# Rounding the next stage's first weights inside the stage in front of it, and modulations in six units

## What is computed

```
mod = silu(c) @ w_ada[l] + b_ada[l]                  # 6 x 1024: shift, scale, gate, twice
h   = layernorm(x) * (1 + sc1) + sh1
proj = h @ w_in                                      # attention, GLA, convolution and gate parts
y = (g_att * att(..) @ w_att_o + g_gla * gla(..) @ w_gla_o + g_conv * conv(..) @ w_conv_o) @ w_out
x = layernorm(ALPHA * x + g1 * y)
x = layernorm(ALPHA * x + g2 * ffn(layernorm(x) * (1 + sc2) + sh2))
```

## Time and profile before

| | |
|---|---|
| median of the runs | 2996.16 us |
| the profiled execution, its span | 3002.65, 3000.9 us |
| PE busy | 2813.7 us (94%) |
| DVE, ACT, POOL busy | 1306.7, 1310.4, 1382.3 us |
| granted TensorE clock, mean | 0.976 |
| read from HBM | 355.51 MB |

### The profile page before, as it was taken

How to read it: one execution, slowest core, us unless ns; L and a number is a source line. 1 busy time by engine, 2 the same in 40 slices (tenths; PEclk the granted TensorE clock), 3 DMA queues, 4 the chain that set the end, 5 groups by cost and what they waited for, 6 DMA issues and landing times.

```text
span 3000.9 us, 45357 instructions
## 1 busy us (share of the span) xinstructions
PE 2813.7 (94%) x19004; PEld 2414.5 (80%) x19004; DVE 1306.7 (44%) x2717; ACT 1310.4 (44%) x2204; POOL 1382.3 (46%) x646
## 2 busy tenths in 40 slices
PE   7999998899999999998999999999998899988998
PEld 5778876688876788886878799989986799876898
DVE  3777857532333211104676753332137442174440
ACT  3254433323424422224464346454454465445563
POOL 3432030244431534443531267668762488632786
PEclk9999999999998999999999999999999999998999
DMA  6332022132324343334320245435543255432454
GB/s 237 121 106 81 29 78 82 46 119 92 119 84 157 121 139 128 119 99 166 124 71 22 64 133 156 148 129 182 182 120 120 78 183 175 137 121 84 137 180 123
DMA packets 103555, 359.48 MB, mean 120 GB/s; under 512 B 11127, under 2 KB 17527, under 8 KB 102841
## 3 DMA queue, kind: packets, MB, share of 16 engines
q1 hardware_dynamic: 103352, 356.60, 37.0%
HBM read 355.51 MB, written 1.05 MB: 119 GB/s over the span
## 4 chain that ended last, share of the span: by engine, by line
PE 79%; DVE 9%; ACT 6%; POOL 3%; DMA 1%; issue 1%; SPq 0%; ACTq 0%; DVEq 0%
PE PS L358 79%; POOL RINGL L2516 2%; ACT AR L1161 2%; DVE AR L1795 1%; ACT AR L1690 1%; ACT WH L1141 1%; DVE AR L1799 1%; DMA RING<-w_ada_in 1%; ACT L1161 1%; DVE AR L1956 1%; DVE SM L1795 1%; ACT XT L1161 1%; DVE SM L2029 1%; DVE AR L2400 1%; DVE ARR L1795 1%
## 5 line engine op out<-in xcount | busy, mean ns | idle before, releaser
L2516 POOL TENSOR_TENSOR RINGL<-RING,WH 128x1024 fp32r<-128x1024 f32 (+1 forms) x554 | 1300.7, 2361 | 1507.3 <-ACT WH L1141 1506.6
L358 PE MATMUL PS<-HTR,WH 128*128 128x256 f32 (+2 forms) x2736 | 876.0, 321 | 0.0
L1141 ACT ACTIVATE WH<-RING 128x1024 fp32r<-128x1024 f32 (+1 forms) x554 | 568.6, 1035 | 643.2 <-PE PS L358 518.5
L358 PE MATMUL PS<-HTH,WH 128*128 128x256 f32 (+1 forms) x2336 | 748.3, 322 | 25.8 <-POOL RINGL L2516 20.6
L358 PE MATMUL PS<-HTH,RINGL 128*128 128x256 f32 (+1 forms) x2336 | 727.2, 317 | 4.1 <-POOL RINGL L2516 4.1
L358 PE MATMUL PS<-ARR,WH 128*128 128x256 f32 (+2 forms) x2688 | 691.8, 325 | 16.5 <-ACT WH L1141 5.8
L358 PEld LDWEIGHTS PS<-HTR,WH 128*128 128x128 f32 (+1 forms) x2736 | 524.1, 192 | 40.2 <-issue 2.1
L358 PEld LDWEIGHTS PS<-ARR,WH 128*128 128x128 f32 (+1 forms) x2688 | 467.3, 191 | 63.2 <-issue 15.2
L358 PEld LDWEIGHTS PS<-HTH,WH 128*128 128x128 f32 x2336 | 449.4, 192 | 66.5 <-issue 20.5
L358 PEld LDWEIGHTS PS<-HTH,RINGL 128*128 128x128 f32 x2336 | 444.7, 192 | 33.6 <-POOL RINGL L2516 5.4
L358 PE MATMUL PS<-ARR,RINGL 128*128 128x256 f32 (+1 forms) x1472 | 466.3, 327 | 1.5 <-POOL RINGL L2516 1.5
(11 more groups left out here) (195 smaller groups left out, 3395.5 us busy)
## 6 DMA issues: line engine op xcount, KB each, us to landing
RING<-w_ada_in SPq DMA_DIRECT2D x96, 512.0 KB, 3.7
RING<-w_up_in SPq DMA_DIRECT2D x88, 512.0 KB, 4.2
RING<-w_gates_in SPq DMA_DIRECT2D x48, 512.0 KB, 3.6
RING<-w_ff_gate_in SPq DMA_DIRECT2D x44, 512.0 KB, 3.7
RING<-w_ff_up_in SPq DMA_DIRECT2D x44, 512.0 KB, 3.6
RING<-w_glu_in SPq DMA_DIRECT2D x32, 512.0 KB, 4.5
RING<-w_ff_down_in SPq DMA_DIRECT2D x32, 512.0 KB, 3.5
RING<-w_in_in SPq DMA_DIRECT2D x32, 512.0 KB, 3.6
```

What stands on the lines that cost most here:

```text
L358: return e.matmul(out_, lhsT, rhs, start=start, stop=stop)
L1141: e.activation(RINGS[name][:, j, 0:width], RING[:, b % NSLOT, 0:width], ACT.Copy).then_inc(*a_upper.up(b))
L2516: e.tensor_tensor(RINGL[:, i, 0:width], RING[:, i, 0:width], RINGS[name][:, j, 0:width], ALU.subtract).then_inc(*g_lower.up(b))
```

## The change

Modulations: six units u = a // 4, each for 16 groups of 128 features, over the same 24 fills; a fill now takes two of the eight input parts for 1024 x 2 output columns, accumulates over four fills in one PSUM bank, and every fourth fill turns the unit before it. `w_ada` is laid out for that on the host. The turn matrix PICK has 8 columns. Roundings: at six places blocks of the next stage are rounded inside the stage in front.

```diff
 def ada_rows(a):                                      # PE
-    o = bank(6 + a % 2 if a < 4 or a >= 12 else 6, "ada", a, until=(a_ada, "row", a))
+    u = a // 4
+    if a % 4 == 0:
+        bank(7 if u == 4 else 6, "ada", u, until=(a_ada, "row", u))
...
+    for k in (2 * (a % 4), 2 * (a % 4) + 1):
+        for half in range(2):
+            n, w, _ = load(A["w_ada"][u // 3, 16 * (u % 3) + 2 * k + half, :, :], 1024, False)
+            for j in range(2):
+                c = 64 * half + 32 * j
+                t = mm(o[c:c + 32, :], SCP[:, k, :], w[:, 512 * j:512 * j + 512], k == 0, k == 7)
 def ada_turn(u):
-        t = mm(o[:, 2 * j:2 * j + 2], ROW[a % 2][:, 128 * j:128 * j + 128], FOLD2, True, True)
+        t = mm(o[:, 8 * j:8 * j + 8], ROW[u % 2][:, 128 * j:128 * j + 128], PICK, True, True)
 def fill(n):
-        if a - 2 >= lo:
-            ada_turn(a - 2)
+        if a % 4 == 1 and a - 1 > lo:
+            ada_turn(a // 4 - 1)
 def layernorm(...):                                   # PE, at its end
+    if nid == ("m", 1, 1):
+        fill_all()
 gla_outputs:                                          # PE
     if i == units + 1:
+        fill(1)
         ring("WH1")
-        fill(1)
 end of layer 0:                                       # PE
-    fill_all()
     ring("WH0")
     layernorm(("m", l + 1, 1), XT, ...)

 def phase(i, n=3):                                    # ACT
-    uppers(up_at[0] + 2)
+    uppers(up_at[0] + n - 1)
 def fill(n):
-        if a - 1 >= lo:
-            ada_row(a - 1)
+        if a % 4 == 0 and a > lo:
+            ada_row(a // 4 - 1)
 layernorm, behind the square root:                    # ACT
+    if nid == ("m", 1, 1):
+        fill_all()
     if then is not None:
         then()
 attend, behind the copy to ARR:
+    if who == "x" and h in (3, 4, 5):
+        uppers(stage_block["w_gates", l, 0] + h - 3)
 merged:
+    if k == 7:
+        uppers(stage_block["w_out", l, 2])
     act.wait_ge(*d_merge.to("sum", l, 2, k))
 conv_norm, in the loop over its 8 tiles (next_gate[0] is ct + 1 of the merge):
+    if k % 4 == 1:
+        ahead("w_gates", l, 8 + next_gate[0])
 next_inputs:
-    phase(2 * l + 1)
+    phase(2 * l + 1, 2)
 projections2:
     product("w_t0", l, 0)
+    ahead("w_in2", l, FIRST_TILES[0])
 end of layer 0:
     post(l, 2, cols, d_norm.to("mul", "m", l, 2, 7))
-    fill_all()
     modulate(("m", 1, 1), BOTH, 0, 1, HA[0], ..., lambda: phase(2))

 att_projections:                                      # DVE
-        beside(side, 1 if l else 3)
+        if i < len(items):
+            beside(side, 1 if l else 3)
 end of layer 0:
+    modulate(("m", 1, 1), BOTH, 0, 1)
     fill_all()
-    modulate(("m", 1, 1), BOTH, 0, 1)
```

More of the change, by code:

```diff
@@ L450, in ada_rows, with ada_turn @@
             def ada_rows(a):
-                l, g = a // 12, a % 12
-                o = bank(6 + a % 2 if a < 4 or a >= 12 else 6, "ada", a, until=(a_ada, "row", a))
+                u = a // 4
+                if a % 4 == 0:
+                    bank(7 if u == 4 else 6, "ada", u, until=(a_ada, "row", u))
+                o = ps("ada", u)
                 pe.wait_ge(*a_ada.to("silu"))
[L454 to L464, removed]
+                for k in (2 * (a % 4), 2 * (a % 4) + 1):
[4 more added lines that the diff above has]
+                            t = mm(o[c:c + 32, :], SCP[:, k, :], w[:, 512 * j:512 * j + 512], k == 0, k == 7)
+                        t.then_inc(*p_block.up(n))
+                if a % 4 == 3:
+                    p_block.also("ada", u)
+            def ada_turn(u):
+                o = take("ada_turn", u, until=(d_ada, "mod", u))
+                pe.wait_ge(*a_ada.to("row", u))
                 for j in range(4):
-                    t = mm(o[:, 2 * j:2 * j + 2], ROW[a % 2][:, 128 * j:128 * j + 128], FOLD2, True, True)
-                t.then_inc(*p_ada.up("turn", a))
+                    t = mm(o[:, 8 * j:8 * j + 8], ROW[u % 2][:, 128 * j:128 * j + 128], PICK, True, True)
+                t.then_inc(*p_ada.up("turn", u))
             def fill(n):
@@ L1142, in uppers, with phase @@
                         *a_upper.up(b))
-            def phase(i):
+            def phase(i, n=3):
                 up_at[0] = phases[i][0]
                 up_end[0] = phases[i + 1][0] if i + 1 < len(phases) else len(blocks)
-                uppers(up_at[0] + 2)
+                uppers(up_at[0] + n - 1)
             def ahead(*label):
@@ L1161, in copy, with ada_row @@
                 return e.activation(out_, in_, f, bias=bias, scale=scale)
[L1163 to L1167, removed]
+            def ada_row(u):
+                act.wait_ge(*p_block.to("ada", u))
+                if u >= 2:
+                    act.wait_ge(*p_ada.to("turn", u - 2))
+                copy(ROW[u % 2], ps("ada", u)).then_inc(*a_ada.up("row", u))
             def fill(n):
@@ L1178, in fill_all @@
                 fill(100)
-                ada_row(ada_at[2] - 1)
+                ada_row(ada_at[2] // 4 - 1)
             def root(r, in_, done):
@@ L1210, in modulate @@
                     layernorm(nid, HT, cols, done, then)
-                act.wait_ge(*d_ada.to("one", 12 * l + 2 * scale + 1))
+                act.wait_ge(*d_ada.to("one", 3 * l + scale // 2))
                 p, c = norm_parts(nid, cols)[0]
@@ L1441, in merge @@
                 for ct in range(8):
+                    next_gate[0] = ct + 1
                     product("w_gates", l, 8 * branch + ct)
@@ L1803, in stt, with ada_mod @@
                 return e.scalar_tensor_tensor(out=out_, in0=a, scalar=s, in1=b, op0=op0, op1=op1)
[L1805 to L1814, removed]
+            def ada_mod(u):
+                l, c = u // 3, 16 * (u % 3)
+                b = COL_AT["b_ada", l] + c
+                dve.wait_ge(*p_ada.to("turn", u))
+                tt(MOD[:, l, c:c + 16, :].rearrange("p (i j) n -> p i j n", i=4),
+                   ps("ada_turn", u)[:, 0:32].rearrange("p (j i n) -> p i j n", i=4, n=2),
+                   bc(COL[:, b:b + 16].rearrange("p (i j) -> p i j", i=4), 3, 2), ALU.add).then_inc(
+                       *d_ada.up("mod", u))
+                scales = {0: 8, 2: 32}.get(u % 3)
+                if scales is not None:
+                    m = MOD[:, l, scales:scales + 8, :]
+                    dve.wait_ge(*d_ada.to("mod", u))
+                    ts(m, m, 1.0, None, ALU.add).then_inc(*d_ada.up("one", u))
             def fill(n):
@@ L1819, in fill @@
                     if a < hi:
-                        if a - 2 >= lo:
-                            ada_mod(a - 2)
+                        if a % 4 == 1 and a - 1 > lo:
+                            ada_mod(a // 4 - 1)
                         ada_at[0] += 1
@@ L1858, in affine @@
                     if c.start == XA.start:
-                        dve.wait_ge(*d_ada.to("one", 12 * l + 2 * scale + 1))
+                        dve.wait_ge(*d_ada.to("one", 3 * l + scale // 2))
                         dve.wait_ge(*d_norm.to("mul", *part(nid, k, p)))
```

18 lines of the change are left out of this document (9 added, 9 removed).

## The result

The changed kernel took 2965.07 us (median; 2963.47 to 2966.27), the kernel before 2995.51 on the same chip: ratio 0.9889, 95% interval [0.9876, 0.9903]. The two medians by themselves give 0.9898, so the gain is 30.4 us by the medians and 33 by the ratio on record. The forecast was 2967, from 2953 to 2982. The profiled execution took 2964.30 us (span 2962.5) against 3002.65, so 38.4 us less, where the medians give 30.4.

What follows compares the result with a forecast made beforehand. PE bounds the kernel (79% of the chain), waiting most for POOL's lower halves. Terms summed to 23.2 us, with the clock 29.2: 2973.5 for the profiled execution, 2967 for the median, range 2953 to 2982.

Steps and rivals of the forecast that it cites:

- The signs: Listed trace evidence: 48 matmuls on ROWS, fill wait about 4.7, two scalings over 2 us, PE gap near 10 us.
- Turns, -10.8: All modulation places: 24 turns become 6, each priced at 0.87 us inside dense PE work; -10.8 us together.
- GLA to attention, -3.1: Layer 0, end of GLA: the 5.09 us wait goes, but the row copy queued behind roundings delays the fill; -3.1 us.
- Taps, -2.9: Layer 0, before attend c: without DVE's convolution taps in the last three rounds, most of PE's 3.25 us wait goes; -2.9.
- Attention, -0.4: Attention to merge, layer 0: the 3.94 us wait and half clock go, two held scalings cost +4.4; net -0.4 us.
- The alternative worked out beside it: Attention to merge: if DVE starts before POOL, the price is one 0.5 us delay of POOL, net -6.
- Convolution norm, -3.2: Layer 1's convolution norm: w_gates a+2 rounded after two silu/copy pairs, 1.9 us earlier, cutting waits of 2.86 and 1.33; -3.2.
- w_out and w_in2, -6.6 and their clock: Joints to w_out and w_in2, both layers: earlier roundings remove waits, -3.3 each; half-clock stretches behind them priced under clock.
- Clock, -6: Half-clock stretches behind the gaps of convolution norm, w_out and w_in2, worth 8.5 us: -6, between 0 and -8.5.
- part 4: Attention to merge, layer 0: half-clock stretch removed, -1.7, but a new one possible from PE's grown gaps, +1.2.
- Layer joint, +4.7: Layer 0 to 1: -4.0 from moving fill_all, but no first block rounded early, PE starts 8.7 later; net +4.7.
- waits that only change their name: Rival: behind each joint the next wait takes half of 16 us, no clock given back; 2981, chance 0.19.

Runs made afterwards that it cites:

- units alone: The kernel before with the modulations alone changed (units of four groups, fill_all moved into the layer joint), none of the roundings: 2991.82 us, ratio 0.9987.
- The run with POOL second: Changed kernel with one wait added: POOL's lower halves of w_gates 0 and 1, layer 0, begin only after DVE's 128x512 scaling; 2962.25 us, 0.9888.
- the short idle-matmul run: Changed kernel with 40 idle matmuls, 33 more than before, in PE's 8.63 us gap at the joint of the layers: 2966.45 us, 0.9904.

## Why the prediction held, step by step

- **The sum**: 29.2 forecast, 30.4 by the medians, 33 by the ratio. That it came so near is in part luck: the norm, the layer joint and the attention missed by 1.3 to 1.7 us in both directions, and places that were priced at nothing add up to -3.9 in the profiles. Of the 38.4 between the profiles, 4 are, as argued above, the late DMA issue. Setting the profile's sum against the profile and the median apart, as was done, was right; taking the 6.5 us between them for a constant was not.
- **The signs**: all four came: 48 matmuls on ROWS, the wait at the fill (4.39, forecast about 4.7), two scalings of 2.35, and the gap of 8.63 with WH behind the eighth tile copy.
- **Turns, -10.8**: units alone, layer joint counted in, gave -4 (-0.6 to -7), forecast -6.1; the trace has each turn in dense work at 0.5 to 0.9. Right, a little high in the feed-forward.
- **GLA to attention, -3.1**: -4.0. The order in ACT's queue and the wait's new place (forecast about 4.7, found 4.39) were right; the clock, counted at nothing, was the rest.
- **Taps, -2.9**: the undoing gives +2.6 at the place.
- **Attention, -0.4**: -2.1. Two held scalings, none at head 5, as foreseen, but at 1.86 each and not 2.2; and the stretch of half clock charged at +1.2 did not come. The alternative worked out beside it, -6 if DVE came first, failed by 0.28 us: POOL was first. That the price was near 2.2 is in part luck: it was taken from one pair of scalings, and it is what is left of POOL's operation when DVE arrives. The Trainium skill ("SBUF — State Buffer", section "SBUF: two separate sides") calls the shared port pair "an **exclusive lock**, not a bandwidth split" for whoever starts first. The run with POOL second agrees, as to DVE held until POOL's end; the changed kernel's trace agrees as to POOL held by DVE (2.85 us in place of 2.36 at 886.22, last section).
- **Convolution norm, -3.2**: the one step that failed. The first gap shrank (2.86 to 1.03), but the second grew from 1.33 to 2.75. The step priced the rounding alone and forgot that PE, 1.8 us earlier, then meets the end of ACT's chain with its table loads. -1.9 was measured, and earlier rounding still brings nothing.
- **w_out and w_in2, -6.6 and their clock**: undone together they cost +16 (traces: +11.9). With two thirds of the clock the sum had 6.6 + 4.5 = 11.1 for them, with the whole of it 13.4. The trace has 10.6 at the joints, as the half clock came back at three of the four; the time would allow either, so these runs do not show that the clock term was too small. In layer 1 a wait for w_out 3's lower half, 2.08 us at 1900.53, is left, which the step had not seen.
- **Clock, -6** (and -1.7 + 1.2 in part 4): in the 36 runs on record of the kernel before, time and granted clock go together, from 3005.16 us at a mean of 0.974 to 2992.43 at 0.981, some 1.3 us for 0.001. The mean over the runs is 0.978 for the kernel before and 0.983 for the changed one; by that slope 6 to 7 us of the gain are clock (an estimate, and a correlation only). The two profiles differ by more, 50 us of PE's busy time at half clock, and that is where a pair of single executions can mislead. In the changed kernel's profile no half clock stands behind w_out of layer 0 or either w_in2; in layer 1's w_out one does, at 1901.7, behind the new wait of 2.08.
- **Layer joint, +4.7**: +3.2; the loss alone 9.0, forecast 8.7, shown by mending it (-8.7 in the trace).
- **Rivals**: waits that only change their name did occur, in DVE's copies (5.0 us by the waits view) and in the norm (1.4), but for 6 us rather than 14, and the clock was given back.

## What to carry to other kernels

When work moves ahead in an in-order queue, list what stood behind its new place: here a 0.6 us row copy behind 5 us of roundings cost 4.4 us, and a phase marker ahead of four blocks of another kind cost 8.7. Put the helper engine's long operations under stretches where its neighbour reads PSUM only, and count the half clock behind each gap that goes, but only as far as the next wait is not fixed by another engine. If a gain at a joint is to last, look at the first wait behind it before the edit: the short idle-matmul run won 1.7 us and lost them 9 us later.

## What the runs showed of the hardware that I had not expected

- Small DVE operations of one tensor are not held by POOL: a scaling and a reciprocal of 128x1 took 0.15 us each at 534.60 and 534.67, inside POOL's operation of 534.58, while the 128x512 scaling of 534.86 was held to POOL's end. Size alone does not decide: a tensor_tensor of 128x2 with both inputs in SBUF took 2.15 us at 2241.17, to the end of POOL's operation of 2240.74, where others of its form take 0.16.
- POOL is held by DVE as well: a lower half that began at 886.22, with 0.58 us of a DVE operation with two SBUF inputs to go, took 2.85 us in place of 2.36; two more, at 889.03 and 1525.12, took 2.84 and 2.85 in the same position. The rows are of the changed kernel:

```profile
884.63 2.17 DVE L1819 SCALAR_TENSOR_TENSOR XT<-XT,AR 128x512 f32<-128x512 f32 x1 [0.98 <-ACT AR L1166]
...
886.22 2.85 POOL L2536 TENSOR_TENSOR RINGL<-RING,WH 128x1024 fp32r<-128x1024 f32 x1
...
2241.17 2.15 DVE L1811 TENSOR_TENSOR SM<-SM,AR 128x2 f32<-128x2 f32 x1
```

- SyncE's issue of one 512 KB transfer mostly takes 0.33 to 0.44 us and now and then 0.9 to 1.8 (the longest, near 3.7 us of each run, aside: 1.9 to 4.5); one such seems to have cost 4 us of a profiled execution.
- Idle matmuls of 128 columns in f32, back to back, took 0.227 us each at full clock (two instructions each in the trace), and the clock stayed at 1.00 through 15 us.
